# A diffusion step on one core: the conv layer's loads and order rearranged, one chunk of the conv moved from VectorE to ScalarE and GpSimd

## What is computed

```python
def conv_module(h, w1, b1, wdw, bdw, gn, w2, b2):
    u = h @ w1 + b1
    a, gt = jnp.split(u, 2, axis=-1)
    u = a * jax.nn.sigmoid(gt)
    dw = depthwise_conv(u, wdw, taps=31) + bdw        # one filter of 31 taps a channel
    return jax.nn.silu(rms_norm(dw, gn)) @ w2 + b2

for i in range(2):
    sh1, sc1, g1, sh2, sc2, g2 = split(silu(cond) @ ada_w[i] + ada_b[i], 6)   # for c_ctx and for c
    y = y + g1 * mixer(modulate(y, norm_mix[i], sh1, sc1))
    y = y + g2 * moe(modulate(y, norm_ffn[i], sh2, sc2), ...)
```

## Time and profile before

| | us |
|---|---|
| median of 3 runs (1443.53 to 1444.20) | 1444.04 |
| the profiled execution, its own time | 1444.01 |
| its span | 1442.2 |
| PE busy | 1365.5 |
| DVE busy | 456.4 |
| ACT busy | 294.1 |
| POOL busy | 0.2 |
| bytes moved | 499.45 MB |

### The profile page before, as it was taken

How to read it: one execution, slowest core, us unless ns; L and a number is a source line. 1 busy time by engine, 2 the same in 40 slices (tenths; PEclk the granted TensorE clock), 3 DMA queues, 4 the chain that set the end, 5 groups by cost and what they waited for, 6 DMA issues and landing times.

```text
span 1442.2 us, 19700 instructions
## 1 busy us (share of the span) xinstructions
PE 1365.5 (95%) x7466; PEld 796.9 (55%) x7466; DVE 456.4 (32%) x1451; ACT 294.1 (20%) x611; POOL 0.2 (0%) x4
## 2 busy tenths in 40 slices
PE   5799689999999999999989989999999999999996
PEld 3576566554555555555534577655555555555553
DVE  0698443222222222222124534322222222222212
ACT  2211241111111111111121333111211111111111
POOL 0000000000000000000000000000000000000000
PEclk8799899999999999999999989999999999999998
DMA  8989664699999999999995528368999999999990
GB/s 306 379 317 355 250 263 177 260 388 405 416 409 410 415 400 415 411 415 412 412 417 213 212 113 324 149 289 359 413 417 407 415 411 403 419 408 407 418 409 33
DMA packets 80641, 499.45 MB, mean 346 GB/s; under 512 B 10633, under 2 KB 15409, under 8 KB 23760
## 3 DMA queue, kind: packets, MB, share of 16 engines
q1 hardware_dynamic: 80592, 498.79, 85.3%
HBM read 497.45 MB, written 1.31 MB: 346 GB/s over the span
## 4 chain that ended last, share of the span: by engine, by line
PE 91%; DVE 5%; DMA 2%; ACT 1%; issue 1%; SPq 0%; DVEq 0%; ACTq 0%
PE ps L829 32%; PE ps L861 16%; PE ps L802 10%; PE ps L871 9%; PE ps L556 4%; PE ps L602 3%; PE ps L630 3%; PE ps L756 2%; PE ps L531 2%; PE ps L841 2%; PE ps L545 1%; DMA ring<-in_conv_w_dram 1%; DVE W L1270 1%; DVE hb L1270 1%; PE ps L849 1%; PE ps L789 1%
## 5 line engine op out<-in xcount | busy, mean ns | idle before, releaser
L829 PE MATMUL ps<-ring,hT 128*64 128x512 f32 x2048 | 453.3, 594 | 1.5 <-ACT hT L1128 0.4
L829 PEld LDWEIGHTS ps<-ring,hT 128*64 128x64 f32 x2048 | 163.6, 137 | 284.4 <-issue 280.0
L861 PE MATMUL ps<-ring,W 128*64 128x512 f32 x1024 | 233.8, 598 | 1.0 <-DVE W L1535 1.0
L1541 DVE TENSOR_TENSOR ypart<-ps,ypart 128x512 fp32r<-128x512 f32 x132 | 91.3, 692 | 191.2 <-ACT ypart L1140 191.2
L802 PE MATMUL ps<-hot,h_hi 128*128 128x256 f32 x544 | 146.8, 304 | 4.0 <-DVE hot L1506 3.3
L1530 DVE SCALAR_TENSOR_TENSOR vec<-silu_h,W,ps 128x256 f32<-128x256 f32 x66 | 31.7, 481 | 355.3 <-ACT silu_h L1134 355.3
L871 PE MATMUL ps<-comb,ypart 128*128 128x256 f32 x1056 | 138.0, 283 | 2.8 <-DVE ypart L1541 2.8
L871 PEld LDWEIGHTS ps<-comb,ypart 128*128 128x128 f32 x1056 | 131.3, 192 | 6.2 <-DVE ypart L1541 4.6
L802 PE MATMUL ps<-hot,h_lo 128*128 128x256 f32 x544 | 134.4, 281 | 0.0
L802 PEld LDWEIGHTS ps<-hot,h_hi 128*128 128x128 f32 x544 | 103.1, 189 | 56.5 <-issue 55.4
L861 PEld LDWEIGHTS ps<-ring,W 128*64 128x64 f32 x1024 | 67.8, 136 | 119.6 <-issue 109.6
(11 more groups left out here) (200 smaller groups left out, 964.3 us busy)
## 6 DMA issues: line engine op xcount, KB each, us to landing
ring<-in_exp_w_gate_dram SPq DMA_DIRECT2D x128, 1024.0 KB, 8.4
ring<-in_exp_w_up_dram SPq DMA_DIRECT2D x128, 1024.0 KB, 10.6
ring<-in_exp_w_down_dram SPq DMA_DIRECT2D x128, 1024.0 KB, 10.2
S<-in_ada_w_dram SPq DMA_DIRECT2D x32, 1024.0 KB, 9.2
ring<-in_ada_w_dram SPq DMA_DIRECT2D x16, 1024.0 KB, 17.6
ring<-in_conv_w_dram SPq DMA_DIRECT2D x4, 2048.0 KB, 18.8
S<-in_attn_wqkv_dram SPq DMA_DIRECT2D x1, 6144.0 KB, 25.5
ring<-in_conv_w_dram SPq DMA_DIRECT2D x1, 4096.0 KB, 21.0
```

The costliest lines, as they stand in the source:

```text
L829: mm = pe.matmul(PGU[64 * b:64 * b + 64, :].rearrange("p (h f) -> p h f", h=2), xg[:, block_of(layout, k), 64 * b:64 * b + 64], gate_up_of ...
L861: mm = pe.matmul(bank[64 * b:64 * b + 64, :], hidT[:, j, 64 * b:64 * b + 64], down_of(w[b])[:, j, n * 512:(n + 1) * 512], start=(j == 0), ...
L1541: dve.tensor_tensor(half_of(1, h), bank[:, :], half_of(0, h), ALU.subtract).then_inc(dve_ylo[l], 1)
```

## The change

**Loads.** The conditioning vectors and the eight small row loads go to ACT's DMA queue; SP starts with the constants and the tokens. Units 0 to 7 get a place each (units 6 and 7 in the ring), so that none of them waits. `conv_w1` comes in six loads: 1 MB, 1 MB (chunks 0 and 1), 1 MB, 1 MB (2 and 3), 2 MB, 2 MB (4 to 7). `conv_w2` comes after unit 19. Units 24 to 31 go into the ring after the diagonal products. Shared expert, one extra, expert 3 and then experts 0 to 2 follow.

**The start's order.** PE multiplies units 0 and 1, then sums the squares, then units 2 to 6, then the rows, then unit 7. DVE normalises before third 0 is there and only scales and shifts after it (`affine`).

**The conv.** The chunks go in their own order. Chunk 5 is the one by diagonals, after all eight inputs. Chunk 1 is convolved without PE and DVE: ACT makes 31 products of `upad` and a tap (L1056), GpSimd adds them in two chains (L1260), 29 additions and one that joins the chains. DVE convolves chunks 0, 2, 3, 4, 6 and 7. Units 20 to 23 are multiplied between the sum of squares and `project`, units 24 to 27 after it, 28 to 31 after the next norm's sum; thirds 1, 2 and 3 are finished one by one, third 3 in the midst of the routing.

```diff
-PE_CHUNK = 3
+PE_CHUNK, POOL_CHUNK = 5, 1
...
+            def products(first, last):
+                act.wait_ge(cv_in, POOL_CHUNK + 1)
+                for j in range(first, last):
+                    if j >= 10:
+                        act.wait_ge(cv_added, j - 9)
+                    o = product[j if j < 2 else 2 + j % KC].rearrange("p (g t) -> p g t", g=G)
+                    x, tap = upad[:, POOL_CHUNK, :, j:j + T], dwc[:, POOL_CHUNK, j:j + 1]
...
+                        if n >= 3:
+                            products((0, 6, 13, 20, 26)[n - 3], (6, 13, 20, 26, TAPS)[n - 3])
...
+        @block.gpsimd
+        def _(pool):
+            for j in range(2, TAPS):
+                pool.wait_ge(cv_product, j + 1)
+                if j >= 4:
+                    pool.wait_ge(cv_added, j - 3)
+                o = product[j % 2]
+                pool.tensor_tensor(o, o, product[2 + j % KC], ALU.add).then_inc(cv_added, 1)
+            pool.wait_ge(cv_added, TAPS - 2)
+            pool.tensor_tensor(product[0], product[0], product[1], ALU.add).then_inc(cv_added, 1)
...
-                    for n, cc in enumerate(CONV_ORDER):
-                        if cc == PE_CHUNK:
-                            continue
+                    for n in (0, 2, 3, 4, 6, 7):
+                        if n == POOL_CHUNK + 1:
+                            gated(POOL_CHUNK)
                         gated(n)
```

More of the change, by code:

```diff
@@ L67, in unit_slot @@
 def unit_slot(u):
+    if u < KC:
+        return u if u < 6 else u + 9
+    if u < 3 * KC:
+        return (u - KC) % 6
     if u < EARLY:
-        return u % 6
+        return 6 + u - 3 * KC
     v = u - EARLY
-    return 6 + (v if v < 9 else v - 9)
+    if v < 9:
+        return 6 + v if v < 6 else 8 + v
+    return v - 3 if v < 15 else 14
 def unit_before(u):
@@ L245, in build_kernel @@
         odd = hb_f[:, 2560:2816]
+        product = [dwo[:, POOL_CHUNK, :], hb_f[:, 2816:3072]] + [sq[:, k, :] for k in range(KC)]
         arow = hT[:, 0:6, :].rearrange("p k t -> p (k t)").rearrange("p (b n) -> p b n", b=3)
@@ L396, in _, with load_w1 @@
             sp.dma_start(xtok[:, 1, :], x_sample[0]).then_inc(ld_x, 16)
[L397 to L404, removed]
-            load_ada(range(KC))
[L406 to L415, removed]
+            def load_w1(part, first, last):
+                for h in range(2):
+                    sp.dma_start(w1[:, :, h * D + first * P:h * D + last * P],
+                                 conv_w1[0].rearrange("(k p) n -> p k n", p=P)[:, :, h * D + first * P:h * D + last * P]
+                                 ).then_inc(ld_w1[part], 16)
+            load_ada(range(KC))
+            load_w1(0, 0, 2)
+            load_w1(1, 2, 4)
+            load_w1(2, 4, 8)
+            load_ada(range(KC, 2 * KC))
             def load_small(dst, src):
@@ L428, in _ @@
                 if l == 0:
+                    load_ada(range(2 * KC, 2 * KC + 4))
+                    sp.wait_ge(x_tr, 4)
+                    sp.wait_ge(ada_used, KC)
+                    sp.dma_start(w2, conv_w2[0].rearrange("(k p) n -> p k n", p=P)).then_inc(ld_w2, 16)
+                    load_ada(range(2 * KC + 4, 3 * KC))
                     sp.wait_ge(cv_u, KC)
                     sp.wait_ge(cv_pe, 1)
+                    load_ada(range(3 * KC, EARLY))
+                    sp.wait_ge(ada_used, 3 * KC)
+                    load_shared(0)
+                    load_extra(0, 0)
+                    sp.wait_ge(pj_out, 4)
+                    load_expert(0, 3, 3, "gu")
+                    load_expert(0, 3, 3, "dn")
+                    sp.wait_ge(ada_used, EARLY)
+                    for s in (0, 1, 2):
+                        load_expert(0, s, s, "gu")
+                        load_expert(0, s, s, "dn")
                 else:
@@ L541, in sum_squares @@
             def sum_squares(n, bank):
-                for k in range(KC):
-                    pe.wait_ge(sq_ready, KC * (n - 1) + k + 1)
-                    mm = pe.matmul(ps[bank][:, 0:TT], ones, sq[:, k, :], start=(k == 0), stop=(k == KC - 1))
+                for i, k in enumerate(SUM_ORDER if n == 2 else range(KC)):
+                    pe.wait_ge(sq_ready, KC * (n - 1) + i + 1)
+                    mm = pe.matmul(ps[bank][:, 0:TT], ones, sq[:, k, :], start=(i == 0), stop=(i == KC - 1))
                 mm.then_inc(ss_ready, 1)
@@ L602, in _ @@
                                 mm = pe.matmul(ps[3 + n % 4][:, h * TT:(h + 1) * TT],
-                                               w1[:, k, h * D + cc * P:h * D + (cc + 1) * P],
+                                               w1[:, k, h * D + n * P:h * D + (n + 1) * P],
                                                hT[:, k, :], start=(k == 0), stop=(k == KC - 1))
                         mm.then_inc(cv_u, 1)
[L606 to L619, removed]
+                    def conv_by_diagonals():
+                        pe.wait_ge(cv_diag, 1)
+                        pe.wait_ge(cv_in, PE_CHUNK + 1)
+                        for j in range(TAPS):
+                            mm = pe.matmul(ps[7][:, 0:TT].rearrange("p (g t) -> p g t", g=G),
+                                           diag(j), upad[:, PE_CHUNK, :, j:j + T],
+                                           start=(j == 0), stop=(j == TAPS - 1))
+                        mm.then_inc(cv_pe, 1)
@@ new lines, in _ @@
+                    conv_input(0)
+                    pe.wait_ge(rows_in, 1)
+                    for n in range(1, 6):
+                        conv_input(n)
+                        if n >= 2:
+                            ada_products(range(KC + 2 * n - 4, KC + 2 * n - 2), ps[1])
+                    conv_input(6)
+                    ada_products(range(2 * KC, 2 * KC + 2), ps[2])
+                    conv_input(7)
+                    conv_by_diagonals()
+                    ada_transposes(1, ps[1])
@@ L972, in squares @@
                 for k in range(KC):
[L973 to L976, removed]
+                    act.wait_ge(ready, value(k))
                     act.activation(sq[:, k, :], src[:, k, :], ACT.Square).then_inc(sq_ready, 1)
@@ L1000, in _, with build_diagonals @@
                 if l == 0:
-                    for n, cc in enumerate(CONV_ORDER):
+                    def build_diagonals(first, last):
+                        for j in range(first, last):
+                            ins = act.activation(diag(j), ident, ACT.Identity, scale=dwc[:, PE_CHUNK, j:j + 1])
+                        if last == TAPS:
+                            ins.then_inc(cv_diag, 1)
+                    def products(first, last):
+                        act.wait_ge(cv_in, POOL_CHUNK + 1)
+                        for j in range(first, last):
+                            if j >= 10:
+                                act.wait_ge(cv_added, j - 9)
+                            o = product[j if j < 2 else 2 + j % KC].rearrange("p (g t) -> p g t", g=G)
+                            x, tap = upad[:, POOL_CHUNK, :, j:j + T], dwc[:, POOL_CHUNK, j:j + 1]
+                            if j == 0:
+                                ins = act.activation(o, x, ACT.Identity, scale=tap,
+                                                     bias=cch[:, 2, POOL_CHUNK:POOL_CHUNK + 1])
+                            else:
+                                ins = act.activation(o, x, ACT.Identity, scale=tap)
+                            ins.then_inc(cv_product, 1)
+                    for n in range(KC):
                         act.wait_ge(cv_u, n + 1)
@@ L1008, in _ @@
                         act.activation(sgt[:, n % 2, :], ps[3 + n % 4][:, TT:2 * TT], ACT.Sigmoid,
[L1009 to L1016, removed]
@@ L1017, in _ @@
-                    act.wait_ge(cv_pe, 1)
-                    act.activation(dwo[:, PE_CHUNK, :], ps[7][:, 0:TT], ACT.Identity,
-                                   bias=cch[:, 2, PE_CHUNK:PE_CHUNK + 1]).then_inc(cv_pe_out, 1)
-                    act.wait_ge(cv_u, KC)
-                    for e in range(1, 4):
-                        ada_copy(e, ps[e % 3])
-                    squares(dwo, 2, cv_out, lambda k: k + 1 if k < PE_CHUNK else k)
+                                       bias=cch[:, 1, n:n + 1]).then_inc(cv_gate, 1)
@@ new lines, in _ @@
+                        if 1 <= n <= 3:
+                            build_diagonals(11 * (n - 1), min(11 * n, TAPS))
+                        if n >= 3:
+                            products((0, 6, 13, 20, 26)[n - 3], (6, 13, 20, 26, TAPS)[n - 3])
+                    ada_copy(1, ps[1])
+                    load_table(ACT.Sqrt)
+                    act.wait_ge(cv_added, TAPS - 1)
+                    done = 0
+                    for k in SUM_ORDER:
+                        if k == PE_CHUNK:
+                            act.wait_ge(cv_pe, 1)
+                            act.activation(dwo[:, k, :], ps[7][:, 0:TT], ACT.Identity,
+                                           bias=cch[:, 2, k:k + 1]).then_inc(cv_pe_out, 1)
```

(10 more changed lines are left out.)

152 lines of the change are left out of this document (86 added, 66 removed).

## The result

| | before | after |
|---|---|---|
| median | 1444.12 us (4 runs) | 1430.08 us (4 runs, 1429.64 to 1431.02) |
| ratio, 95% interval | | 0.9901 (0.9884 to 0.9918) |
| span of the profiled execution | 1442.2 us | 1429.2 us |

The change takes 14.0 us off, where 6.3 us were forecast. The direction was right and the main mechanisms were there, but two terms of the sum were mis-sized: the start gained 2.3 us more than forecast, and GpSimd's additions cost 4.6 us less.

A forecast was written before the change was run, and what follows sets the result against it. DVE's work was taken to bound 57 to 154 us, with PE's order adding 4.5 us, and the DMA queue the start. Sum: 1444.0 - 5.7 - 16.8 + 16.8 - 1.0 + 0.5 = 1437.8 us; range 1419 to 1447 us.

The forecast's parts named there:

- The start: Up to PE's first conv product: 40.9 us instead of 46.6 us, 5.7 us earlier, bounds nothing and 12.8 us.
- the hole at 23 to 27 us: DMA engines 0.18 busy at the start; one of 16 engines is behind, so the gain is smaller than the hole.
- the 0.9 us by which unit 7 was to come earlier: Loads at the start: two issues of some 0.45 us no longer ahead of the tokens, unit 7 at 34.8 us.
- The conv without GpSimd: DVE's six chunks, first gate to last step, GpSimd's effect left out: 79.9 us, 16.8 us less.
- PE's order: DVE's one idle at 114.6 us, behind an input PE made after diagonals and four ada units: 4.5 us less.
- The additions: GpSimd's 30 additions beside DVE's conv steps, at 0.56 us each: 16.8 us more, ends 0 and 52 us.
- each addition costs DVE its own length: Conv: DVE and GpSimd exclude each other; length 0.43 to 0.69 us, middle 0.56 us.
- Behind the conv: After DVE's last step: hand-over unchanged, `project` 1.0 us less (0 to 3.1), third 3's turn 0.5 us more.
- No contention: Conv: GpSimd's additions leave DVE alone, 1421.0 us; chance 22%.
- Dear additions: Conv: additions cost DVE enough to be slower than before, 1448 us at 0.9 us each; chance 13%.
- the larger start: Start: the taps no longer hold one engine back, 7.1 us more gain, 1430.7 us; chance 8%.
- The start without gain: Start: ACT's queue takes its turn from SP's, `conv_w1` lands as late as before, 1443.5 us; chance 7%.

The follow-up runs named there:

- experiment 3: The changed kernel with the taps' 31 rows loaded as 16 and 15 rows instead of in one load: 1428.2 us.
- experiment 4: The changed kernel with the eight small row loads back on SP's queue, behind the tokens and ahead of the units: 1433.5 us.
- Experiment 2: The changed kernel with chunk 1 back on DVE, no ACT products and no GpSimd additions, seven chunks of taps: 1429.1 us.
- experiment 1: The changed kernel with DVE's two running sums of every chunk in a PSUM bank instead of SBUF: 1418.3 us, ratio to before 0.9819.
- experiment 6: The changed kernel with GpSimd adding only 128 of each product's 256 columns, half of chunk 1's sums left out: 1422.0 us.
- experiment 5: The changed kernel with ada units 20 to 23 multiplied before the conv's sum of squares instead of between it and `project`: 1431.7 us.

## Why the prediction was wrong, step by step

**The start** was forecast at -5.7 us and was -8.0 us. The reading of the hole at 23 to 27 us was right: one engine behind, so that the slots cost less than they seem to (experiment 3). The step that failed is the 0.9 us by which unit 7 was to come earlier. It counted only the two issues ahead of the tokens, and nothing for the eight row loads that moved to ACT's queue, since they run "over the same 16 engines". Unit 7 came 3.0 us earlier (at 32.8 us, not 34.8 us), and experiment 4 gives 1.5 us of that to the rows being off SP's queue. The remaining 0.8 us of the start are not settled.

**The conv without GpSimd** was sized right: 91.9 us less the 12.2 us by which the three chunks are too long is 79.7 us, forecast 79.9 us. PE's order gave its 4.5 us, as the gap of the earlier trace rows before 114.62 us is gone. Experiment 2, whose DVE never meets GpSimd, needs 91.7 us for seven chunks.

**The additions** were forecast at +16.8 us and cost 12.2 us; this is the largest miss, 4.6 us. The mechanism was right for the tap steps: two SBUF inputs against GpSimd's reads, as experiments 1 and 6 show. Wrong was the step "each addition costs DVE its own length". An addition takes 0.73 us undisturbed but holds a tap step for only 0.47 us. In the timeline 21 tap steps are longer (not 26, as the expectation of experiment 1 has it), together 9.9 us; the rest is two joins and four of the products that begin a chunk. Over 30 additions the 12.2 us are 0.41 us each, below my bounds of 0.43 and 0.69 us, which came from DVE rows and described neither the addition nor what DVE loses by it. That the miss is not larger is luck: with an addition's real length the same step would have given 30 x 0.73 = 21.9 us.

The rule of the Trainium skill that stood beside the sum (SBUF — State Buffer, Who interferes with whom: an instruction with two SBUF inputs contends with a GpSimd instruction that reads SBUF) agrees with the traces. Its other half, that the loser blocks for the whole of the other instruction, does not: DVE lost 0.47 us to an addition of 0.73 us. The two estimates of an addition's price worked out from the Trainium skill (GPSIMD Engine Reference, Performance versus the Vector engine), 0.56 us and 0.83 us, lie on either side of the 0.73 us of an undisturbed addition, and both are above what DVE lost.

**Behind the conv** I had `project` 1.0 us shorter; it became 2.9 us shorter, and the hand-over, forecast unchanged, 2.1 us longer. The sum (-0.9 us) is near the forecast by luck, since both halves are off: I priced four units at their warm 3.6 us, but PE was at the lower clock there (0.50 in 140 to 146 us) and took 5.6 us, and it is this work that brought the clock up for `project` (experiment 5). The 0.5 us for the turn were there (0.44 us in the chain), and the stretch was still 0.2 us shorter.

**The rivals.** No contention would have been 1421.0 us; experiment 1 removes the contention and gives 1418.3 us, so that rival's price was nearly right and its condition false. Dear additions did not come. Of the larger start 2.3 of its 7.1 us came, but not by its condition: the taps still held an engine back (experiment 3). The start without gain did not come.

## What to carry to other kernels

- Work given to GpSimd beside a busy VectorE is not free when both read two tiles from SBUF. Count the meetings and price them by what the addition reads, or take one of VectorE's inputs out of SBUF: a running sum in a free PSUM bank cost 0.13 us a chunk here and gave 12 us.
- A gap in the DMA share need not be worth its length. See what share is left in it: here it was 0.06, one engine, and a load with few rows was ahead on it.
- Before a long product, a little work on TensorE can pay for itself by the clock, if it fits in a wait that is there anyway.

## What the runs showed of the hardware

- An addition of 128x256 fp32 on GpSimd, undisturbed: 0.73 us, one every 0.69 us (experiment 1); of 128x128 0.45 to 0.53 us (experiment 6).
- Beside VectorE steps with two SBUF inputs: one of each every 0.87 us, where VectorE alone does one every 0.40 us. A step that reads one tile from SBUF and one from PSUM keeps its length (0.48 us), also when it writes to SBUF; a product of one SBUF tile and a scalar, written to SBUF (L1355), does not (0.82 us instead of 0.35 us).
- While steps with two SBUF inputs follow each other at 0.40 us, an addition that comes late may wait: such additions took 3.7, 4.6 and, in experiment 6, 8.1 us. All three ended beside VectorE's join. I had expected turns from the first meeting on. The join is another kind of instruction, and it also starts 0.51 us after the last step instead of 0.40 us; which of the two lets the addition in is not shown. What decides whether it gets in at once, as at 81.27 us, or waits, stays open.
